# A tuned two-block kernel with its work area moved by 64 bytes in each SBUF partition

## The reference, cut to what matters

```python
def hybrid_layer(x, norm_g, w_in, conv_w, w_out_a, ..., w_glu, b_glu, w_out_b, w_o):
    h = rmsnorm(x, norm_g)
    proj = jnp.einsum('bld,dn->bln', h, w_in)            # 2048 x 14336
    v, bg, cg, za, u, zb, ga, gb = jnp.split(proj, SPLITS, axis=-1)
    ya = bg * causal_depthwise_conv(cg * v, conv_w)
    ya = jnp.einsum('blc,cd->bld', ya * jax.nn.silu(za), w_out_a)
    yb = jax.nn.gelu(s5_scan(u, ...))                    # 64 groups of 64 complex states
    yb = yb * jax.nn.sigmoid(jnp.einsum('blc,ce->ble', yb, w_glu) + b_glu)
    yb = jnp.einsum('blc,cd->bld', yb * jax.nn.silu(zb), w_out_b)
    m = jax.nn.sigmoid(ga) * ya + jax.nn.sigmoid(gb) * yb
    return x + jnp.einsum('bld,de->ble', m, w_o)
```

## Time and profile before

| | before |
|---|---|
| median of 3 runs | 2267.07 us (2261.08 to 2267.31) |
| profiled execution | 2267.02 us, its span 2265.3 us |
| mean granted TensorE clock | 0.993 |
| busy: TensorE, VectorE, ScalarE, GpSimd | 98%, 69%, 46%, 12% |
| weight loads, beside the matmuls | 96% |
| matmuls | 20,556 |
| read from HBM | 384.29 MB, 171 GB/s over the span |

### The profile page before, as it was taken

The page is one execution under the profiler, slowest core; times in us unless marked ns, Lnnn a source line. Parts: engine busy times, 40 slices in busy tenths (PEclk is TensorE's granted clock), DMA queues, the critical chain, the costliest instruction groups (busy, mean ns, idle before and its releaser), DMA issues.

```text
span 2265.3 us, 51607 instructions
## 1 busy us (share of the span) xinstructions
PE 2219.6 (98%) x20556; PEld 2163.5 (96%) x20556; DVE 1568.1 (69%) x2060; ACT 1040.4 (46%) x1357; POOL 265.0 (12%) x178
## 2 busy tenths in 40 slices
PE   7999999999999999999999999899999999999997
PEld 7999999999999989999999788799999999999997
DVE  7799989889545667778766577676666666654444
ACT  6544444444544444566344344554444444443443
POOL 0344444444100000100011000000000000000000
PEclk9999999999999999999999899999999999999999
DMA  7555555555555555555555011255555555556553
GB/s 262 177 170 181 176 180 176 177 178 186 189 191 185 187 196 193 189 177 174 201 176 181 29 49 49 77 186 186 185 186 185 186 186 185 185 180 190 183 181 136
DMA packets 107104, 387.81 MB, mean 171 GB/s; under 512 B 12032, under 2 KB 12160, under 8 KB 106752
## 3 DMA queue, kind: packets, MB, share of 16 engines
q1 hardware_dynamic: 104400, 375.44, 50.8%
q0 software_dynamic: 2176, 9.78, 1.3%
q10 hardware_dynamic: 432, 1.21, 0.1%
HBM read 384.29 MB, written 2.10 MB: 171 GB/s over the span
## 4 chain that ended last, share of the span: by engine, by line
PE 92%; DVE 4%; ACT 2%; issue 1%; DMA 0%; DVEq 0%; SPq 0%; ACTq 0%
PE ps_main L1691 28%; PE ps_main L1693 27%; PE ps_main L1692 27%; PE ps_aux L1919 2%; DVE w_lo L977 1%; PE ps_main L1919 1%; PE ps_main L1990 1%; ACT w_hi L495 1%; PE ps_aux L1940 1%; DMA w_raw<-wmain 0%; PE ps_main L1992 0%; PE ps_main L1991 0%; PE ps_aux L1760 0%; PE ps_aux L1748 0%; PE ps_main L1964 0%
## 5 line engine op out<-in xcount | busy, mean ns | idle before, releaser
L977 DVE TENSOR_TENSOR w_lo<-w_raw,w_hi 128x1024 fp32r<-128x1024 f32 x718 | 918.3, 1295 | 459.1 <-ACT w_hi L495 453.8
L495 ACT ACTIVATE w_hi<-w_raw 128x1024 fp32r<-128x1024 f32 x718 | 747.4, 1046 | 739.6 <-PE ps_main L1693 729.6
L1691 PE MATMUL ps_main<-xs,w_hi 128*128 128x256 f32 x1664 | 467.8, 281 | 2.7 <-DVE w_lo L977 1.8
L1692 PE MATMUL ps_main<-xs,w_hi 128*128 128x256 f32 x1664 | 464.5, 279 | 0.0
L1693 PE MATMUL ps_main<-xs,w_lo 128*128 128x256 f32 x1664 | 464.2, 279 | 0.0
L1691 PE MATMUL ps_main<-x3s,w_hi 128*128 128x256 f32 x1408 | 394.4, 280 | 0.0
L1693 PE MATMUL ps_main<-x3s,w_lo 128*128 128x256 f32 x1408 | 392.8, 279 | 0.0
L1692 PE MATMUL ps_main<-x3s,w_hi 128*128 128x256 f32 x1408 | 392.8, 279 | 0.0
L1691 PEld LDWEIGHTS ps_main<-xs,w_hi 128*128 128x128 f32 x1664 | 312.4, 188 | 9.5 <-DVE w_lo L977 5.0
L1693 PEld LDWEIGHTS ps_main<-xs,w_lo 128*128 128x128 f32 x1664 | 312.6, 188 | 0.0
L1692 PEld LDWEIGHTS ps_main<-xs,w_hi 128*128 128x128 f32 x1664 | 311.4, 187 | 0.0
(11 more groups left out here) (420 smaller groups left out, 3777.1 us busy)
## 6 DMA issues: line engine op xcount, KB each, us to landing
w_raw<-wmain SPq DMA_DIRECT2D x622, 512.0 KB, 3.4
w_raw<-wdown SPq DMA_DIRECT2D x80, 512.0 KB, 3.7
w_raw<-wdown SPq DMA_DIRECT2D x16, 256.0 KB, 2.7
bias<-bias POOLq DMA_DIRECT2D x8, 384.0 KB, 3.4
x_res<-xt POOLq DMA_DIRECT2D x4, 512.0 KB, 6.5
out<-x_res SPq DMA_DIRECT2D x3, 512.0 KB, 2.8
x_first<-xt SPq DMA_DIRECT2D x2, 512.0 KB, 7.1
x_first<-xt ACTq DMA_DIRECT2D x2, 512.0 KB, 9.4
```

The source lines that it names most:

```text
L495: nc.scalar.activation(whi[:, s, 0:width], raw[:, s, 0:width], ACT.Copy).then_inc(hi_ready, 1)
L977: V.tensor_tensor(wlo[:, s, 0:width], raw[:, s, 0:width], whi[:, s, 0:width].bitcast(F32), ALU.subtract)\
L1691: nc.tensor.matmul(out, whi[:, s, w], high[:, k, :], start=(first and kk == 0), stop=False)
L1692: nc.tensor.matmul(out, whi[:, s, w], low[:, k, :], start=False, stop=False)
```

## The change

The work area starts 64 bytes later in each partition. Everything that `wk` places moves with it; the ring, `x_res`, `par`, `const` and the tiles of the `small` area keep their places. No instruction is added, removed or reordered.

```diff
@@ -157,7 +157,7 @@
         gg = at("gg", small + 14 * K, [KB])
         phi = at("phi", small + 14 * K + 64, [STATE_TILES])
         rho = at("rho", small + 14 * K + 192, [STATE_TILES])
-        work = small + 14 * K + 320
+        work = small + 14 * K + 384
 
         def wk(name, kb, shape, dtype=F32):
             assert base + work + kb * K + 4 * int(np.prod(shape)) <= nc.sbuf_usable_end, name
```

## The result

The changed kernel takes 2279.4 us (median of 4, 2278.49 to 2282.89) where the kernel before took 2266.38 (median of 4): 1.0065 times as long, 95% interval 1.0046 to 1.0084 (the ratio is estimated from all runs and not from the two medians). By the medians it is slower by 13 us, more than the 0.3% that a measurement can tell. Executions of one kernel lie some 6 us apart with their mean granted clock (the kernel before, on one chip: 2257.5 to 2262.7 us at 0.994 to 0.996, 2266.8 to 2268.3 us at 0.992 and 0.993), and the two profiled executions, both at 0.993, took 2267.02 and 2282.89 us, so the change costs some 16 us. The forecast was 2267 and no change.

The account below looks back on a forecast made before the run. TensorE was taken as the bound, large matmuls times their start-to-start pitch. TensorE distances, other engines and transfers each added zero, leaving 2267 us; range 2260 to 2274 for no change, 2194 to 2326 with the rivals.

Parts of the forecast that it names:

- no change: Whole kernel: the forecast outcome, 2267 us, own range 2260 to 2274, chance 0.42.
- The bound and the count: TensorE bounds the span: 17,040 large matmuls times the pitch (start to next start), 117.8 ns, give 2007 of 2265.3 us.
- the cost of the new distance: TensorE's moving operand against weight blocks: distances 320 and 832 modulo 1024 become 384 and 896, claimed to cost nothing.
- the 290 ns of the first stage: L1692 matmuls on `x_raw_l` last 280 and 290 ns by turns; read as distance 512 cheap, 0 dear.
- The natural experiment: First stage: `x_raw_l`, outside the work area at distances 0 and 512; 356.6 ns per three matmuls against 353.4 in steady stretch.
- Slower: Rival: distance 896 as dear as 0, 6.4 ns on 8,520 large matmuls, 55 us more, 2322 us; chance 0.31.
- Faster: the cadence changes: Rival: the large matmuls move to the 113.3 ns cadence seen in some stretches, 71 us less, 2196 us; chance 0.27.
- The pitch isn't set in SBUF: Rival: 117.8 ns comes from instruction issue, so distances don't show; 2267 us, chance included in the 0.42 of no change.
- The second and third parts: VectorE, ScalarE and GpSimd accesses to moved tiles, and transfers landing 64 bytes further on: zero each; engines bounded by 9 us.

Follow-up runs that it names:

- the added restarts: Two small matmuls put behind each of the second, third and fourth ffn columns: on the changed kernel 2281.96 us (one run); on the kernel before 2238.64 us, ratio 0.9893.
- the table: Work area and act tile moved to other offsets against the kernel before: ratios from 0.9926 (both at 704) to 1.0065 (both at 384); 2293.87 us at 352 / 416.

## Why the prediction was wrong

**The bound and the count** were right. The span is 17,040 large matmuls times a pitch; nothing but the pitch moved, and by the rule that I set (wrong if it moves by more than 0.4 ns) it moved by 0.89. The 2279.4 us lie inside the wide range of 2194 to 2326, which the bounds of the rivals had set, but outside the 2260 to 2274 of "no change".

**The step that failed** is the cost of the new distance, "I take the nearer row for both: no cost". It rested on two readings. The first was that distances count modulo 1024, so that 384 lay between cheap 320 and cheap 512. They count modulo 256: 512 is 0, the dearest multiple of 64, and 384 is 128, the second dearest of them. The second was that the 290 ns of the first stage belong to distance 0 and the 280 to distance 512. Both are 0 modulo 256; the alternation is a rhythm of two triples, as the whole kernel moved by 64 bytes showed by changing foot. The natural experiment was a true sign that the distance matters, and it gave the right order of magnitude for the mean (118.9 against 117.78 with one operand of two at 0), but I divided it into a dear and a cheap half that don't exist.

**The rivals.** "Slower" had the right sign and the wrong mechanism: not 10 ns on every second matmul, 55 us, but 0.89 ns on all. "Faster: the cadence changes" had the wrong sign, but its mechanism is the one that the runs bore out. There are two cadences at one layout, and which one is caught is decided at a restart; but at 128 modulo 256 the second one is slower, no fast one appeared with or without the added restarts, and the change took away the 90 us of it that there were. "The pitch isn't set in SBUF" is ruled out by the table: programs that differ in addresses alone have slow pitches of 117.33 to 120.0 ns; the 113.33 beside them is a matter of the restart.

The Trainium skill (SBUF — State Buffer, "Who interferes with whom") gives PE two independent read ports and says that it never waits on anyone. Taken as a forecast of the time, that fails for this kernel: seven programs, alike but for addresses, gave four pitches without the fast cadence and five with it. Which access waits, if one does, no run shows.

**The second and third parts**, other engines and transfers, cost nothing, as forecast. VectorE's busy time is 1567.2 after 1568.1 us, ScalarE's 1040.9 after 1040.4. ScalarE's wait for TensorE grew with the span, from 729.6 to 743.2 us:

```profile
ACT w_hi L495 <- PE ps_main L1693: 743.2, 449, 5.2
```

## What to carry to other kernels

Where TensorE is the bound and its large matmuls each load new weights, look at the pitch in a long steady stretch and compare it between stages: two values for the same instructions mean that something can be had. Then move the moving operands against the weights by multiples of 64 bytes; here 192 modulo 256 was best, and 0 worst of these, where it was tried in one stage. The whole scale, 113.3 to 120 ns, is 6% of the pitch; between whole kernels the most that was measured is 0.9837 against 1.0065 of the time before. And a steady state can have two cadences: a break at the right moment may be worth more than the work it costs, so look at what the restart of a long stretch caught before blaming its code. The runs don't say how to choose that moment; the pairs here were tried, not aimed.

## What had not been expected of the hardware

- The pitch in the steady state depends on the distance between moving operand and weights modulo 256 bytes: 120.00 ns at 0, 117.78 or 113.33 at 64 and 192, 118.67 or 120.00 at 128; 120.0 at 96 and 117.33 at 160 (one run). In cycles of 2.4 GHz these are 288 (120.00), 282.7 (117.78), 272 (113.33) and 284.8 (118.67).
- These are 18, 17 2/3, 17 and 17.8 times 16 cycles, which invites the thought of reads in pieces of 64 bytes, 16 columns, that wait for one another. It wasn't tested, and single intervals from start to start don't fit it: in the changed kernel most are 115, 119, 120 or 122 ns, where 16 cycles are 6.67 ns. Which stream meets which load is open too, since the run with w_lo moved met neither pairing.
- At 64, 128 and 192 modulo 256 there are two cadences at one layout, and a stretch has the one that it keeps by its third triple behind an interruption. At 0 only 120.00 ns was seen, in one stage of two kernels.
- Six small matmuls more, some 2 us of work (0.74 us a pair, from the pair's start to the second L1691 behind it, less one triple), made the kernel 24 us faster, by what the second pair did to the rhythm of the 6,000 that follow.
